# Constant matmuls in the waits of the second network's attention, and three instead of four early output tiles

## The reference

```
u = rmsnorm(h); proj = u @ w_in
a_out = sparse attention, 8 heads of 64: a top-64 selection of keys by an indexer, bias by distance, softmax
b_out = differential attention, 4 heads with two softmax maps each, then rmsnorm
c_out = silu(gc) * rmsnorm(retention), 4 heads: (q k^T * decay) v, no softmax
h = h + concat(a_out, b_out, c_out) @ w_out
h = h + square(relu(rmsnorm(h) @ w_ff1)) @ w_ff2
```

## Time and profile before

| | us |
|---|---|
| median of 3 runs | 2277.7 |
| the profiled execution's own time | 2270.6 |
| its span | 2268.7 |
| TensorE (PE) busy | 2127.3 (94%) |
| GpSimd (POOL) busy | 1167.2 (51%) |
| VectorE (DVE) busy | 1047.7 (46%) |
| ScalarE (ACT) busy | 904.5 (40%) |
| mean granted TensorE clock | 0.963 |

### The profile page before, as it was taken

The page is one execution under the profiler, slowest core; times in us unless marked ns, Lnnn a source line. Parts: engine busy times, 40 slices in busy tenths (PEclk is TensorE's granted clock), DMA queues, the critical chain, the costliest instruction groups (busy, mean ns, idle before and its releaser), DMA issues.

```text
span 2268.7 us, 34434 instructions
## 1 busy us (share of the span) xinstructions
PE 2127.3 (94%) x12552; PEld 1776.8 (78%) x12552; DVE 1047.7 (46%) x1922; ACT 904.5 (40%) x1553; POOL 1167.2 (51%) x888
## 2 busy tenths in 40 slices
PE   6999999999999998998999999888999998978997
PEld 3666666778887888777899988765999987648997
DVE  3088776454333235997677144245320242454201
ACT  3222433244333234244466443343453333434542
POOL 1332232525444555343789845330788744406995
PEclk8999999999999999999999999896999998979999
DMA  9787221327232333332555734220555543204653
GB/s 389 283 333 251 70 61 46 116 86 159 95 93 93 98 97 107 88 102 85 149 162 181 236 116 122 83 66 10 150 177 177 157 147 93 84 19 123 193 187 111
DMA packets 115653, 306.07 MB, mean 135 GB/s; under 512 B 29848, under 2 KB 44440, under 8 KB 115284
## 3 DMA queue, kind: packets, MB, share of 16 engines
q1 hardware_dynamic: 112984, 297.94, 41.2%
q10 hardware_dynamic: 2556, 6.55, 1.6%
HBM read 300.06 MB, written 8.06 MB: 136 GB/s over the span
## 4 chain that ended last, share of the span: by engine, by line
issue 51%; POOL 40%; PE 7%; POOLq 1%; DVE 0%; DMA 0%; ACT 0%
POOL w_lo L574 40%; PE bank L1031 2%; PE bank L1033 2%; PE bank L1032 2%; POOLq L570 0%; POOLq L578 0%; DVE rinv L1633 0%; DVE nb L1641 0%; DVE rinv L1646 0%; DMA out_x<-nb 0%; PE bank L1082 0%; DVE H L1633 0%; ACT sq L643 0%; POOLq L574 0%; ACT rinv L630 0%
## 5 line engine op out<-in xcount | busy, mean ns | idle before, releaser
L574 POOL TENSOR_TENSOR w_lo<-raw,w_hi 128x512 fp32r<-128x512 f32 x884 | 1167.0, 1347 | 1080.2 <-ACT w_hi L597 1079.6
L597 ACT ACTIVATE w_hi<-raw 128x1024 fp32r<-128x1024 f32 x442 | 466.0, 1055 | 315.9 <-PE bank L1033 250.1
L1031 PE MATMUL bank<-h_hi,w_hi 128*128 128x512 f32 (+1 forms) x1216 | 423.8, 349 | 8.0 <-POOL w_lo L574 4.3
L1032 PE MATMUL bank<-h_lo,w_hi 128*128 128x512 f32 (+1 forms) x1216 | 419.0, 345 | 0.0
L1033 PE MATMUL bank<-h_hi,w_lo 128*128 128x512 f32 (+1 forms) x1216 | 416.9, 343 | 0.0
L1031 PEld LDWEIGHTS bank<-h_hi,w_hi 128*128 128x128 f32 x1216 | 231.2, 190 | 65.0 <-issue 27.4
L1031 PE MATMUL bank<-u_hi,w_hi 128*128 128x272 f32 (+1 forms) x880 | 261.4, 297 | 11.7 <-POOL w_lo L574 4.8
L1032 PE MATMUL bank<-u_lo,w_hi 128*128 128x272 f32 (+1 forms) x880 | 257.3, 292 | 0.0
L1033 PE MATMUL bank<-u_hi,w_lo 128*128 128x272 f32 (+1 forms) x880 | 256.9, 292 | 0.0
L1033 PEld LDWEIGHTS bank<-h_hi,w_lo 128*128 128x128 f32 x1216 | 230.4, 189 | 28.7
L1032 PEld LDWEIGHTS bank<-h_lo,w_hi 128*128 128x128 f32 x1216 | 230.4, 189 | 27.8 <-issue 0.2
(11 more groups left out here) (265 smaller groups left out, 3591.3 us busy)
## 6 DMA issues: line engine op xcount, KB each, us to landing
raw<-in_wstream SPq DMA_DIRECT2D x442, 512.0 KB, 3.6
ada_raw<-in_wada SPq DMA_DIRECT2D x96, 512.0 KB, 6.4
biash<-rpb_by_offset SPq DMA_DIRECT2D x64, 64.0 KB, 3.4
rpb_by_offset<-in_rpb SPq DMA_DIRECT2D x16, 224.0 KB
bias_by_distance<-vec ACTq DMA_DIRECT2D x1, 3264.0 KB
bias<-bias_by_distance SPq DMA_DIRECT2D x2, 1632.0 KB, 8.6
X<-in_x_in ACTq DMA_DIRECT2D x1, 2048.0 KB, 11.7
bias<-bias_by_distance SPq DMA_DIRECT2D x2, 864.0 KB, 6.2
```

The source lines that it names most:

```text
L574: i = pool.tensor_tensor(w_lo[:, s, part], raw[:, s, part], w_hi[:, s, part].bitcast(F32), ALU.subtract)
L597: act.activation(w_hi[:, s, :], raw[:, s, :], ACT.Copy).then_inc(sem("w_hi_ready"), 1)
L1031: pe.matmul(o, hi, a_hi, start=start, stop=False)
L1032: pe.matmul(o, hi, a_lo, start=False, stop=False)
```

## The change

Two constant matmuls go ahead of S for units 14, 15, 17, 18 and 19 (bank 3), two ahead of V for units 0 to 3 (bank 7), four ahead of V for units 18 and 19 (bank 3), and three behind the last T, before the late parts (bank 3). Output tile 3 is no longer begun in step 21 but computed whole behind the late parts of tiles 0, 1 and 2. All of it holds for both layers.

```diff
-        beside += [[("bc_rest", 3), ("mix", 0), ("mix", 1)], [("mix", 2), ("mix", 3)]]
+        beside += [[("bc_rest", 3), ("mix", 0), ("mix", 1)], [("mix", 2)]]
...
+                        if kind == "S" and k in (14, 15, 17, 18, 19):
+                            keep_busy(3, 2)
                         scores2(layer, k)
                     elif kind == "T" and has_values(k):
                         turn2(layer, k)
                     elif kind == "V" and has_values(k):
+                        if k < 4:
+                            keep_busy(7, 2)
+                        elif k >= N_UNITS - 2:
+                            keep_busy(3, 4)
                         values2(layer, k)
...
                 s += L2_FRONT + 8
-                for m in range(RING):
+                keep_busy(3, 3)
+                for m in range(RING - 1):
                     mix2(layer, s, m, MIX_LATE)
-                for m in range(RING, DC):
+                for m in range(RING - 1, DC):
                     mix2(layer, s, m, MIX_EARLY + MIX_LATE)
```

## The result

The changed kernel takes 2280.82 us (median of 20 runs, 2270.72 to 2290.83), the kernel before 2274.84 (20 runs, 2266.76 to 2280.49). The ratio is 1.0029, 95% interval 1.0016 to 1.0042: 6.6 us slower, where a gain of 10 was forecast. The profiled execution has a span of 2278.9 us against 2268.7. That pair alone can't carry the result: 6.2 of its 10.2 us lie ahead of T(0) of layer 0, where both programs are the same.

What follows compares the result with a forecast made beforehand. TensorE, busy 94% of the span, was taken as the bound, losing time in waits and at its lower clock. Front 5.0, scores 0, tiles 0 and 1 2.3, tile 4 3.0 sum to 10.3, taken as 10: about 2268, range 2261 to 2276.

Steps and rivals of the forecast that it cites:

- the clock term of the front: Steps 1 to 13: 13.9 us to win from the lower clock, less 4.6 and 0.7 for falls that remain.
- V(0) and V(1): Constants there fill 0.9 of waits of 1.08 and 1.10 us, delay nothing, and TensorE goes on almost without a pause.
- The 0.7: Front: 0.7 us taken off for half a stretch more, as the waits around S(4) come to lie otherwise.
- V(2) and V(3): Their constants cost 0.9 us a layer each; V(3)'s wait stays, with one clock fall a layer, 4.6 us in all.
- The lower bound of the front: -5.3 us: clock falls as before, 3.6, plus 0.9 for V(3)'s constants at the lower clock and 0.7 for V(1)'s.
- Steps 14 to 19: Constants ahead of S fit into waits or spare time beside VectorE and ScalarE: 0 us, bounds +3 and -1.5.
- My sign that step 14 to 20 would not grow: Trace check: the prediction would be wrong if step 14 to 20 grows; steps 17 to 19 stay as long as before.
- V(18), tiles 0 and 1, tile 4: Late part: tiles 0 and 1 at the higher clock give 2.3 us; no clock fall behind tile 4's wait gives 3.0.
- The second rival: Slower: constants unhidden or at 1.2 GHz from V(1) to V(3) and at V(18), clock as before: 8.5 us, 2286; chance 0.10.
- The first: Rival: the clock falls in front almost as often; the front gives about 0, the rest 4: 2274; chance 0.17.
- The third: Rival: the higher clock only makes TensorE wait longer, VectorE and ScalarE setting the pace in front too: 2278; chance 0.08.

Runs made afterwards that it cites:

- e1: The kernel before with only the pairs of constants ahead of V(0) to V(3): 6.4 us (0.28%) slower than the kernel before.
- e7: The kernel before with only the pairs ahead of V(0) and V(1): 1.1 us faster than before, interval -2 to +5.
- e3: The kernel before with only the pairs ahead of S(14), S(15), S(17), S(18) and S(19): -1.4 us, not clear of zero.
- e2: The kernel before with only the late part (constants ahead of V(18), V(19) and the late parts, tile 3 moved): -2.3 us, not clear of zero.
- e13: The kernel before with only single constants ahead of S(4), S(5), S(7), S(9), S(11) and S(13): 0.21% faster than before.
- e15: The changed kernel plus single constants ahead of S(4), S(5), S(7), S(9), S(11) and S(13): 0.40% (9.1 us) faster than the changed kernel.
- e5: The kernel before with only the pair ahead of V(2): +1.1 us, not clearly different from before.
- e6: The kernel before with only the pair ahead of V(3): +0.5 us, not clearly different from before.
- e8: e4 plus four constants ahead of V(3) (bank 6) and one ahead of S(4), S(5), S(7), S(9), S(11), S(13) (bank 7): 0.14% behind e4.
- e9: e8 with the constant ahead of S(5) in bank 3 instead of bank 7: 2252.93 us, 0.93% less than the kernel before.
- e4: The changed kernel without the pairs ahead of V(2) and V(3): 0.59% or 13.4 us faster than the changed kernel, 0.30% faster than before.
- e14: e4 plus four constants ahead of V(3) in bank 6, nothing in the 0.6 us waits: 2259.60 us, 0.22% ahead of e4.

## Why the prediction was wrong

**The step that failed** is the clock term of the front: of "Front: 13.9 - 3.6 - 4.6 - 0.7 = 5.0 us gained", the 13.9 - 4.6 - 0.7 = 8.6 us to be won back from the lower clock. The runs show none of it: e1 has 166 us at the lower clock, as the kernel before has, and e1 gives -6.4 us in place of +5.0. In the profiles, by the clock means, the first parts of the changed kernel have 0.11 x 2 x 96 + 0.09 x 2 x 90.6 = 37.4 us at the lower clock, against 30.8 before and 5.3/0.45, about 12, forecast. Three things were wrong in the term.

- *V(0) and V(1).* Their pairs delay nothing and the clock stays up behind them, as forecast. I took the stretches behind them for won; in layer 0 the fall came at V(2) instead, and T(0) to T(3) takes 25.1 and 21.2 us with the pairs (e7) and without (e3). Over the runs they bring 1 us, not clear of zero.
- *One execution as the base.* The profile I read had T(0) to T(2) at 18.9 and 16.8 us; e2 and e3, whose front is that of before, have 15.8 and 13.7. And it had no fall from S(6) to S(14), where e3 has 24 us at the lower clock.
- *The short waits.* The 0.7 stood for those around S(4); those of steps 5 to 13 had no term at all. Filling all of these wins 4.8 us in the kernel before (e13) and 9.1 in the changed one (e15). They gave the clock more places to fall than V(3), but e3 falls there too, so they don't explain why the changed kernel is slower than before.

**V(2) and V(3): right in kind, too small.** This is what made the front a loss. Forecast 3.6 us for both layers; their own time in the changed kernel's trace is 6.0, since V(3)'s run as the clock falls, which I had as the lower bound only. The change kept its claim ahead of V(3)'s constants, so the wait of 2.1 us stayed and with it the fall; the prediction saw this and priced it at 4.6 us. (The lower bound of the front, 3.6 + 0.9 + 0.7, is 5.2 and not 5.3.) Taken out of the changed kernel the two pairs give 13.4 us, added alone to the kernel before 1.6 (e5 and e6): why these differ is open.

**Steps 14 to 19: right.** Forecast 0, e3 gives -1.4 us with an interval over zero. My sign that step 14 to 20 would not grow held for S(14) to S(19). In step 18 of the changed kernel VectorE's bias addition still follows the probabilities at once:

```profile
1558.68 0.71 DVE L1644 TENSOR_SCALAR p<-p,small 128x144 f32<-128x144 f32 x3
1559.43 0.62 DVE L1640 TENSOR_TENSOR bank<-bank,bias 128x432 f32<-128x432 f32 x1
```

**V(18), tiles 0 and 1, tile 4: the mechanism was right, the size not shown.** Forecast 2.3 + 3.0; the waits at tile 4 and the fall behind them are gone, tile 0 has the full clock in layer 0 and not in layer 1, and its wait for VectorE grew by 0.9 and 1.1 us, which takes back what an earlier TensorE could win there. e2 gives 2.3 us, with up to 5.7 inside its interval and zero too.

**The second rival** named the right side and place, but by another way: it has the clock as before behind V(0), where it was 1.00. **The first** is what happened to the clock (falls nearly as often), with a front of 0 and not of -6.4. **The third** shows ahead of tile 0, where TensorE's wait grew, and not in the front.

**The Trainium skill's** warning ("TensorE: Matmul & The Clock Gate", "Why this matters for your kernels") concerns idle gaps longer than almost all here; the trace goes further against it than I used: the clock fell behind a wait of 0.63 us, and filling waits of 0.6 us won time (e13).

## What to carry to other kernels

Constants in a wait pay only if they start with the wait: look at what the claim of their bank waits for, since a filler behind the claim that ends the wait is pure cost (e8 against e9: one such constant a layer costs 18 us by the ratios and 13 in the traces). Before counting what a fuller engine wins, read more than one execution: where the clock falls differs from run to run, a stretch that looks safe in one profile may not be, and the mean clock over all runs tells it. Fill all the waits of a stretch in which TensorE is the bound, the short ones too, and leave alone those where other engines set the pace.

## What was not expected of the hardware

The same wait of 0.63 us among small matmuls was followed by a stretch at 1.2 GHz in the changed kernel's profile and not in that of before. Several kernels fell at nearly the same places: 17.4 us behind T(0) of layer 0 in e1, e4 and e14, 3.7 in e2, e3 and e13. And time at the lower clock has very different worth: of 166 us, e8 took 53 away and was 0.16% faster, e9 took 63 and was 0.93% faster.
